# Heads in pairs on halves of the matrix unit, and projections, row jobs and copies in other places, in three transformer blocks on one core

## The reference

```
# first block, two layers
h  = rms_norm(x) * (1 + scale) + shift            # scale, shift, gate = silu(c) @ w_ada
cq, ckv, kr, za, qb, kb, vb, zb, qc, kc, vc, zc, g = split(h @ w_in)
oa = mla(rms(cq) @ w_uq, rms(ckv) @ w_ukv, rope)  # 8 heads, 64 + 32 dims
ob = swa(qb, kb, vb, sink, bias)                  # 8 query heads, 2 key heads, 64 dims
oc = diff(qc, kc, vc)                             # 4 heads, 2 softmaxes of 64 dims each
y  = (sig(g0)*(oa*silu(za)@wo_a) + sig(g1)*(ob*silu(zb)@wo_b) + sig(g2)*(oc*silu(zc)@wo_c)) @ w_out
x  = x + gate * rms_norm(y)
# second block
o1 = window attention with 256 context keys       # 8 heads of 64 dims
o2 = two-way linear recurrence                    # 4 heads of 128, chunks of 32 tokens
x  = x + gate * rms_norm([o1, o2] @ w_out)
x  = x + gate * rms_norm(experts(top 32 tokens of each of 16 experts))
```

## Time and profile before

| | us |
|---|---|
| median of 3 runs | 2578.53 (2577.84 to 2579.51) |
| profiled execution | 2581.11 |
| its span | 2579.2 |
| PE busy | 1953.6 (76%) |
| DVE busy | 527.1 (20%) |
| ACT busy | 285.5 (11%) |
| DMA mean | 277 GB/s |

### The profile page before, as it was taken

One profiled execution on the slowest core, in us unless ns is written; L12 is line 12 of the kernel. 1 busy time (PEld: TensorE's weight loads), 2 busy tenths in 40 slices (PEclk: granted clock), 3 DMA queues, 4 the chain that ended last, 5 costly groups with the idle time before them and its releaser, 6 DMA issues.

```text
span 2579.2 us, 25660 instructions
## 1 busy us (share of the span) xinstructions
PE 1953.6 (76%) x10574; PEld 1092.1 (42%) x10574; DVE 527.1 (20%) x1147; ACT 285.5 (11%) x701; POOL 53.1 (2%) x80
## 2 busy tenths in 40 slices
PE   5899999799999799967666666666666666666565
PEld 1758877576877468633432222221222212212111
DVE  1124322204422315555320001000010000100001
ACT  1112220102220102130100000000000000000000
POOL 0000000000000300002000000000000000000000
PEclk9989999899999899989787878778877778877877
DMA  9533544242445423320669999999999999999996
GB/s 323 162 121 111 179 162 171 75 151 98 164 174 183 151 67 123 137 98 17 264 274 423 423 422 421 422 423 423 423 421 422 423 424 422 422 422 423 423 422 279
DMA packets 149551, 714.92 MB, mean 277 GB/s; under 512 B 11711, under 2 KB 16191, under 8 KB 95904
## 3 DMA queue, kind: packets, MB, share of 16 engines
q1 hardware_dynamic: 143776, 697.08, 67.5%
q0 software_dynamic: 2016, 7.21, 1.1%
q10 hardware_dynamic: 3640, 8.94, 1.0%
HBM read 709.38 MB, written 3.80 MB: 277 GB/s over the span
## 4 chain that ended last, share of the span: by engine, by line
issue 62%; PE 30%; DVE 4%; DMA 2%; ACT 0%; POOL 0%; ACTq 0%; POOLq 0%; DVEq 0%; SPq 0%
PE banks L744 10%; PE banks L1520 4%; PE banks L1529 3%; PE banks L799 1%; PE banks L862 1%; PE banks L749 1%; PE banks L1565 1%; PE banks L795 1%; PE banks L1550 1%; DVE arena L1988 1%; PE banks L885 1%; DMA arena<-in_w_mods_dram 1%; PE banks L1603 1%; PE banks L703 1%; PE banks L808 1%
## 5 line engine op out<-in xcount | busy, mean ns | idle before, releaser
L2196 PE MATMUL banks<-arena 128*32 128x512 f32 (+2 forms) x3072 | 470.3, 741 | 308.7 <-DMA arena<-in_w_up_dram 302.9
L2196 PEld LDWEIGHTS banks<-arena 128*32 128x32 f32 x3072 | 128.8, 137 | 590.7 <-issue 584.1
L744 PE MATMUL banks<-arena 128*128 128x256 f32 x1536 | 344.7, 382 | 0.0
L744 PEld LDWEIGHTS banks<-arena 128*128 128x128 f32 x1536 | 290.3, 192 | 39.8 <-issue 1.7
L2223 PE MATMUL banks<-arena 128*32 128x512 f32 x1280 | 209.3, 792 | 116.0 <-DMA arena<-in_w_down_dram 76.2
L2335 DVE SCALAR_TENSOR_TENSOR arena<-arena,banks 64x512 f32<-64x512 f32 (+1 forms) x48 | 30.5, 635 | 789.6 <-ACT arena L2248 789.0
L2223 PEld LDWEIGHTS banks<-arena 128*32 128x32 f32 x1280 | 46.2, 131 | 260.2 <-issue 258.6
L2248 ACT ACTIVATE arena<-banks 64x512 f32<-64x512 f32 (+1 forms) x48 | 26.6, 555 | 841.3 <-PE banks L2196 834.6
L1520 PE MATMUL banks<-arena 128*128 128x256 f32 x512 | 112.8, 380 | 0.3 <-DVE arena L1843 0.2
L1520 PEld LDWEIGHTS banks<-arena 128*128 128x128 f32 x512 | 96.4, 190 | 14.4 <-issue 0.8
L2342 DVE COPY arena<-banks 128x512 f32<-128x512 f32 x16 | 11.1, 692 | 367.6 <-PE banks L2231 367.6
(11 more groups left out here) (321 smaller groups left out, 1784.3 us busy)
## 6 DMA issues: line engine op xcount, KB each, us to landing
arena<-in_w_gate_dram SPq DMA_DIRECT2D x128, 1376.0 KB, 30.1
arena<-in_w_up_dram SPq DMA_DIRECT2D x128, 1376.0 KB, 32.2
arena<-in_w_down_dram SPq DMA_DIRECT2D x160, 1024.0 KB, 30.4
...
```

Source lines behind the costliest of these rows:

```text
L744: mm = pe.matmul(b[:, i * S:i * S + S], w, rhs[:, kt, :], start=kt == 0, stop=kt == 7)
L2196: mm = pe.matmul(bank[pc][32 * g:32 * g + 32, 0:w_], xsT[:, kt, CAP * e4:CAP * e4 + CAP], (wg if g < 2 else wu)[:, c:c + w_], start=kt == ...
```

## The change

It has these parts.

1. **Pairs of heads.** Scores of two units are issued together in the even ticks, their matmuls in turn: unit t with partitions 0 to 63, unit t+1 with partitions 64 to 127, into the two score banks. Keys are kept without zeros. For mla heads the 96-partition matmuls stay whole and only stand in turn. The wait before the scores is for the exponential (second block: the maximum) of unit t-1 instead of t-2. Values of two units are issued together at the end of the even ticks, in turn for the upper and the lower 64 partitions of the result; diff heads' values stay single. In the second block units are ordered so that a pair is two heads with the same half of the queries.
2. **Keys of the second branch.** `kb` becomes one job of 8 matmuls with 128 columns. After `vb`, two matmuls with shifted identity swap the halves into the same bank, and VectorE copies twice. `vb` becomes one job, and `kr` goes into the job of `ckv`.
3. **Order of the middle jobs.** `rotk`, `q`, `rotq`, `kn`, `v` stand among `qc`, `kc`, `vc`; the loads `w_uq` and `w_ukv` come earlier.
4. **Second block.** The fill keeps `tqh`, `zf`, `zb`, `gh`. The four `ih` jobs come right behind the attention, beside the decay chain, with ScalarE's copies between its logarithms and exponentials; two buffers of the chain move, since `ih` still reads what lay below them. The `mod` and `modT2` jobs come at the ends of the scan's heads. The load of `G2` comes after the last `modT2`. Two zeroings of keys on VectorE (L1846, L1847) go.

The diff, cut to its core:

```diff
+    uq, qc, ukv, kc, vc = (i,), (i + 1, i + 2), (i + 3,), (i + 4, i + 5), (i + 6, i + 7)
+    i += 8
+    jobs += [("rotk", 0, ()), ("q", 0, uq), ("q", 1, uq), ("qc", 0, qc), ("rotq", 0, ()), ("q", 2, uq), ("q", 3, uq),
+             ("qc", 1, qc), ("rotq", 1, ()), ("kn", 0, ukv), ("kn", 1, ukv), ("kc", 0, kc), ("rotq", 2, ()),
+             ("kn", 2, ukv), ("kn", 3, ukv), ("kc", 1, kc), ("rotq", 3, ()), ("v", 0, ukv), ("vc", 0, vc),
+             ("v", 1, ukv), ("vc", 1, vc)]
...
-MODS_AFTER = {"zf": (0, 1), "zb": (2, 3), "ih": (4, 5)}
+ORDER2 = ("qn", "kn", "vn", "qh", "zf", "zb", "gh", "ih")
+MODS_AFTER = {"ih": (0, 1, 2, 3, 4, 5)}
...
+SCAN_MODS = ((("mod", 0), ("mod", 1)), (("modT2", 0), ("mod", 2), ("modT2", 1), ("mod", 3)),
+             (("modT2", 2), ("mod", 4), ("modT2", 3), ("mod", 5)), (("modT2", 4), ("modT2", 5)))
...
+    for z in ("zf", "zb"):
+        jobs += [(z, n, i[z]) for n in range(4)]
+    jobs += [("gh", n, i["gh"]) for n in range(2)]
+    jobs += [("ih", n, i["ih"]) for n in range(4)]
...
+        jobs += [(k, n, i[n] if k == "mod" else ()) for k, n in SCAN_MODS[h]]
...
+FILL2, AFTER_FILL2 = JOB2["tqh", 0], JOB2["ih", 0]
...
+    return 2 * (t // 4) + t % 2, t // 2 % 2
...
+                        one(b[:, 0:S], loads[0], lambda w: w[:, 256:384], hTv)
+                        mm = one(b[NOPE:QK, S:2 * S], loads[0], lambda w: w[:, 384:416], hTv)
...
+                        mm = one(b[:, 0:S], loads[0], lambda w: w[:, 0:P], hTv)
...
-                        pe.wait_ge(exp_done.sem, exp_done.at(l, u - 1))
+                        pe.wait_ge(exp_done.sem, exp_done.at(l, u))
...
+                        for i in range(2):
+                            kind, h, c = UNITS[u + i]
+                            r = slice(64 * i, 64 * i + 64)
+                            if kind == "swa":
+                                q_, k_ = qbv[r, h // 2, a], kbv[r, (h // 4) ^ i, :]
+                            elif kind == "diff":
+                                q_, k_ = qcv[r, h, a], kcv[r, h, :]
+                            else:
+                                q_, k_ = qav[0:QK, h, a], kav[0:QK, h, :]
+                            mm = pe.matmul(SB[i][:, t * S:t * S + S], q_, k_, start=True, stop=True)
+                            if t == 1:
+                                mm.then_inc(s_done.sem, s_done.up())
...
+                    both = (u,) if UNITS[u][0] == "diff" else (u - 1, u)
...
+                        for x_ in both:
+                            kind, h, _ = UNITS[x_]
+                            n, half = TURN[x_], x_ % 2
+                            rows = slice(0, P) if kind == "diff" else slice(64 * half, 64 * half + 64)
+                            v_ = (vbv[:, kt, 64 * (h // 4):64 * (h // 4) + 64] if kind == "swa" else
+                                  vcv[:, kt, h * P:h * P + P] if kind == "diff" else vmv[:, kt, h * 64:h * 64 + 64])
+                            mm = pe.matmul(OBv[rows, m % 2, :], v_, pTv[:, n % 2, kt * S:kt * S + S], start=kt == 0, stop=kt == 1)
+                            if kt == 1:
+                                mm.then_inc(pv_done.sem, pv_done.up())
...
+                job(JOB_OF["kb", 0])
+                job(JOB_OF["vb", 0])
+                pe.wait_ge(kb_ready.sem, kb_ready.at(l, 1))
+                for i in range(2):
+                    mm = pe.matmul(bank[JOB_OF["kb", 0] % BANKS][64 * i:64 * i + 64, S:2 * S], ident[:, 64 - 64 * i:P - 64 * i],
+                                   kbv[:, 0, :], start=True, stop=True)
+                mm.then_inc(kb_swapped.sem, kb_swapped.up())
+                for j in range(JOB_OF["rotk", 0], FIRST_FILL):
...
+                j = JOB_OF["kb", 0]
+                dve.wait_ge(job_done.sem, made(l, j))
+                nc.vector.tensor_copy(kbv[:, 0, :], bank[j % BANKS][:, 0:S]).then_inc(kb_ready.sem, kb_ready.up())
+                dve.wait_ge(kb_swapped.sem, kb_swapped.at(l, 1))
+                nc.vector.tensor_copy(kbv[:, 1, :], bank[j % BANKS][:, S:2 * S]).then_inc(reader(j), 1)
...
+                    if t < NU and t % 2 == 0:
...
+                    if t - 1 in TURN and t % 2 == 0:
...
+                nc.scalar.copy(ckv, bank[j % BANKS][:, 0:S])
+                nc.scalar.copy(kav[NOPE:QK, 0, :], bank[j % BANKS][NOPE:QK, S:2 * S]).then_inc(reader(j), 1)
...
-        Kb2, CS2 = [Kb, xn], [CS, at(e0, 2048)]
+        Kb2, CS2 = [vna, xn], [nab[:, 2048:4096], at(e0, 2048)]
...
-
+                    if kind == "gate3" and n == 0:
+                        pe.wait_ge(reader(JOB2["modT2", 5]), taken(L2, JOB2["modT2", 5]))
...
+                if t < UNITS2 and t % 2 == 0:
...
-                        pe.wait_ge(mx2.sem, mx2.at(0, t - 1))
...
+                        pe.wait_ge(mx2.sem, mx2.at(0, t))
+                    for c, (q_, k_) in enumerate(((qR2v, kr2v), (qT2v, kc2v))):
+                        for i in range(2):
+                            h, q = unit2(t + i)
+                            r = slice(64 * i, 64 * i + 64)
+                            mm = pe.matmul(SB[i][:, S * c:S * c + S], q_[r, h // 2, q * P:q * P + P], k_[r, h // 2, :],
+                                           start=True, stop=True)
+                            if c == 1:
+                                mm.then_inc(s2.sem, s2.up())
...
+                if t >= 1 and t % 2 == 0:
+                    m = (t - 1) // 4
+                    pe.wait_ge(pt2.sem, pt2.at(0, t))
...
+                        for i in range(2):
+                            u = t - 2 + i
+                            h, q = unit2(u)
+                            mm = pe.matmul(OBv[64 * i:64 * i + 64, m % 2, q * P:q * P + P], vnav[:, (k + 2) % 4, h * 64:h * 64 + 64],
+                                           pTv[:, u % 2, k * P:k * P + P], start=k == 0, stop=k == 3)
+                            if k == 3:
+                                mm.then_inc(pv2.sem, pv2.up())
...
+            for k in range(4):
+                pe.wait_ge(reader(JOB2["ih", k]), taken(L2, JOB2["ih", k]))
...
+                    for kind, n in SCAN_MODS[h]:
+                        job(JOB2[kind, n])
...
+            def values_job(n):
+                out_job(JOB2["ih", n], Vnv[:, n, :], bank2(JOB2["ih", n]))
+
+            values_job(0)
...
+                for n in ((1, 2), (3,))[d]:
+                    values_job(n)
...
-
-                    act.dma_start(G2, A["g_post2_2"].to_broadcast([P, D])).then_inc(row3_in, 16)
                     act.dma_start(xn[:, 0:D], A["b_mod_2"][:, 5 * D:6 * D].to_broadcast([P, D])).then_inc(row3_in, 16)
+                if d == 1:
+                    for kind, n in SCAN_MODS[h]:
+                        if kind == "mod":
+                            j = JOB2[kind, n]
+                            out_job(j, mrow2[:, 512 * (n % 2):512 * (n % 2) + 512], bank2(j))
+            act.wait_ge(job_done.sem, made(L2, JOB2["modT2", 5]))
+            act.dma_start(G2, A["g_post2_2"].to_broadcast([P, D])).then_inc(row3_in, 16)
...
-            pool.wait_ge(qk2.sem, qk2.at(0, 2))
+            pool.wait_ge(job_done.sem, made(L2, JOB2["ih", 3]))
             nc.gpsimd.memset(KC, 0.0).then_inc(vz.sem, vz.up())
             pool.wait_ge(vz.sem, vz.last())
+            for n in range(4):
+                pool.wait_ge(reader(JOB2["ih", n]), taken(L2, JOB2["ih", n]))
...
-            nc.vector.memset(kzr, 0.0)
-            nc.vector.memset(kzc, 0.0).then_inc(z2.sem, z2.up())
-            dve.wait_ge(z2.sem, z2.last())
...
-                nc.vector.tensor_copy(kzcv[0:64, 4 * n:4 * n + 4:2, :], b[0:64])
-                nc.vector.tensor_copy(kzcv[64:P, 4 * n + 1:4 * n + 4:2, :], b[64:P]).then_inc(reader(j), 1)
+                nc.vector.tensor_copy(kc2[:, 512 * n:512 * n + 512], bank2(j)).then_inc(reader(j), 1)
...
+                for kind, n in SCAN_MODS[h]:
+                    if kind == "modT2":
+                        j = JOB2[kind, n]
+                        dve.wait_ge(job_done.sem, made(L2, j))
+                        nc.vector.tensor_reduce(mcv[:, 4 * n:4 * n + 4, :], partial_rows(bank2(j)), AX_X,
+                                                ALU.add).then_inc(reader(j), 1)
...
+            for n in (4, 5):
+                dve.wait_ge(reader(JOB2["modT2", n]), taken(L2, JOB2["modT2", n]))
```

184 lines of the change are left out of this document (57 added, 127 removed).

## The result

| | before | after |
|---|---|---|
| median of the runs, us | 2579.02 (2577.84 to 2580.68, 4 runs) | 2492.2 (2487.14 to 2493.92, 4 runs) |
| ratio, 95% interval | | 0.966 (0.9648 to 0.9672) |
| profiled execution, us (span) | 2581.11 (2579.2) | 2487.14 (2484.7) |
| mean granted clock | 0.871 | 0.877 |

The change takes 86.8 us off, 3.4%. The forecast was 2490, with 89 us taken off. The profiled execution of after is the fastest of its four, so its span is 94.5 us shorter, not 87. The stretches, in the columns of the earlier trace rows: first block ticks, second block ticks, decay chain, scan, and 1238 us of the experts.

What follows compares the result with a forecast made beforehand. TensorE was taken to bound both blocks' ticks, and DMA the experts' fixed last 1238 us. Savings of 50 us in the first block's two layers and 39 in the second, 89 off 2578.5, gave 2490 us, range 2475 to 2514.

Steps and rivals of the forecast that it cites:

- Pairs: First block's ticks, per layer: paired tiles take half the time; swa saves 7.4 us, diff 2.5, mla 4.4, with 2.7 back.
- The exponential of unit t-1: First block's even ticks: the new, later wait for this exponential before the scores was costed at nothing.
- `kb` and `vb`: First block, second branch's keys and values: 15.2 us before, 7.7 after, 7.5 saved a layer.
- Middle: First block, from `q` to first scores: 24.6 us before, rotation and half-clock waits mostly go, 6.3 saved a layer.
- Second block's ticks: 167.0 us become 115.5: work of 106.6 plus 9 of waits, some 1.1 in each of eight z jobs.
- Decay chain: Second block: `ih` jobs fill TensorE's idle time; the copy of `ih` 2 delays exponentials, 0.5 us back.
- Scan: Second block: row jobs and transposes at the head boundaries and end cost 12.8 us.
- `G2`: Load at the scan's end, some 2 us before the expert loads: lands below 8 us, costed at nothing.
- The rival's cost: `G2` waits behind expert loads, landing 27.5 us after the scan's end, gate rows some 19 later: 2509 us, chance 0.05.
- Without overlap on partitions: Rival for score pairs of 64-dim heads: each costs 0.87 us more, 24 pairs, 21 in all: 2511 us, chance 0.14.
- The slow alternations: Rival: alternating tiles drain TensorE each time, 224 alternations; at 0.5 us each 2602 us, chance 0.01.
- Chains that take more: Rival, second block: z ticks lose 2.2 us instead of 1.1, boundaries twice the count: 2511 us, chance 0.13.

Runs made afterwards that it cites:

- experiment 4: Changed kernel, but both units' scores in pairs of 64-row heads read q and k from partitions 0 to 63: 2508.38 us.
- experiment 2: Changed kernel with the four score matmuls of a pair issued unit by unit instead of in turn: 2492.45 us.
- experiment 3: Changed kernel with the first block's middle jobs and their two loads back in the old order, behind qc, kc and vc: 2501.47 us.
- experiment 8: Experiment 7's kernel plus row jobs 3 to 5 behind the scan, G2's load earlier, and the copy of ih 2 behind the exponentials: 2473.49 us.
- experiment 5: Changed kernel with the six row jobs and their transposes back in the second block's ticks, G2's load back beside the first kkT copy: 2493.17 us.
- experiment 7: Changed kernel with five banks for the scan instead of three, next head's kkT ahead of row jobs, last two row transposes behind the scan: 2481.43 us.
- experiment 6: Changed kernel with G2's load moved, three kernels: behind the router's load 2515.19 us; ahead of it, with the expert loads, 2489.2; on GpSimd's queue 2494.52.

## Why the prediction was right

The span got 94.5 us shorter. By the starts of stages in the two traces it divides so: up to layer 0's first scores 15.8; from there to layer 1's 23.2; layer 1's ticks 11.3 and what follows to the second block's scores 0.5; from those to the first `kv` 52.7; the scan -13.4; from its last states to the first expert matmul 4.2; the experts 0.2.

- *What bounds the kernel.* The experts take 1267.9 us before and 1267.7 after from their first matmul, with the same row at full DMA share. The premise held, and the gains ahead of the scan's end came through in full.
- *Pairs.* I took half the time for tiles on different partitions with no row for it, because of the column strips. That was a choice and not a shown price, and it came true: it is half exactly (experiment 4), in both orders that were tried (experiment 2). The ticks of layer 1 lost 196.0 - 184.7 = 11.3 us, the sum 7.4 + 2.5 + 4.4 - 2.7 = 11.6. The waits behind the diff heads (L947) are 0.5 us three times instead of 0.75 nearly four times, and the pairs cost a little more than 0.87: 1.73 for an mla pair of scores, 1.02 to 1.06 with the change of shape for the others.
- *The exponential of unit t-1,* costed at nothing, has no wait in the first block's ticks.
- *`kb` and `vb`:* 7.5 forecast, 15.2 - 7.7 = 7.5 measured.
- *Middle:* the step that failed in size. I took 6.3 a layer; from the end of `vb` (before) or of the swap (after) to the first scores the traces give 66.0 - 61.2 = 4.8, and undoing it costs 4.6 to 4.8 (experiment 3). The waits I listed came out as written (0.34, 0.35 and 0.78). What I had too low is the price of small jobs standing singly among full ones: each `rotq` takes 1.02 to 1.03 us from start to start where I had 0.87, and every q, kn and v piece changes the shape again, where I had written 0.9 for all of it.
- *Second block's ticks:* 113.2 us from 915.44 to 1028.59, forecast 115.5. Matmul work and changes are 109 us, 2 more than summed; the waits are 4 us, not 9. The mechanism (VectorE's reciprocal delays a unit) was right, the place was not: I had taken a loss in every one of the eight z ticks. Most of it (3.1 of 4 us) shows in only two ticks, at the values, by way of ScalarE's queue. That the other ticks lose nothing because a pair's values stand only in every second tick fits the rows, but no run here separates it.
- *Decay chain:* the copy of `ih` 2 was the mechanism, 1.1 us reach the scan (38.0 from the end of the ticks to the first `kv`, 36.9 before) and not 0.5; experiment 8 gets 0.9 of it back. Full clock came as forecast.
- *Scan:* 12.8 forecast, 13.4 measured, with row jobs whole on the path at the boundaries. What I did not weigh is that this gives back nearly all that their leaving the ticks had saved (13.4 of 16.1 by the stages, experiment 5), though my own terms, 12.8 and 13.9, say so; and I did not see that over three quarters of what experiment 7 takes off the scan were waits for a bank.
- *`G2`:* cost nothing, as taken, and landed 3.7 us after issue. The rival's cost is real, 23 us (my price: 19), but not its condition: beside the expert loads `G2` lands in 7.6 us, and only behind the router's load in 28.1 (experiment 6).
- *The other rivals.* Without overlap on partitions the time would have been 2508 (experiment 4; my price 2511). The slow alternations are out: a pair costs no more in turn than by unit. Chains that take more are out by the waits.

The total fits in part because errors of both signs met. Against the 89 of the sum, the span lacks 3 us of the middle in two layers, and 0.6 each of the two layers' ticks, the decay chain and the scan; it has 2.3 more from the second block's ticks, and 7.7 that no step of mine has: 3.5 ahead of layer 0's first scores and 4.2 behind the scan. Most of these 7.7 us are TensorE's clock in the one execution that was profiled, and not edits:

- *Ahead of layer 0's first scores, 3.5.* In before it is 26.3 us from the first `q` to the first scores in layer 0, at a mean granted clock of 0.74, and 24.6 in layer 1, the same code, at 0.86: 1.7 us. The old order does not force it, since the kernel of experiment 3 has 73.8 us from `kb` to the scores in both layers. The other 1.8 lie in the last stretch ahead of `kb`, which took 17.9 us at 0.91 in before and 16.1 at 1.00 in after (in its own layer 1 after took 17.8 at 0.90).
- *Behind the scan, 4.2.* From the router's first matmul to the first expert matmul it is 29.6 us in before and 26.5 in after, 3.1 less; experiment 3, whose code is that of after there, also took 29.6. In both of the longer cases the router's matmuls ran at 0.50 throughout, 7.0 us instead of 4.5. Another 0.9 belongs to the change: the scan's last states took 1.94 us at 0.50 before and 1.09 at 1.00 in after, where row jobs and transposes keep TensorE busy; in experiment 5, without them there, they took 1.94 again.

The median of after lies 5 us above this execution. What stays open is why the same stretch gets one level of the clock in one execution and the other in the next. Over the twelve kernels with this front, layer 0's first scores come between 176.0 and 181.0 us.
